# First modulation in blocks of 256 channels, part of its sums on VectorE, projection 0 started block by block, and the context's modulation vector made apart

## The chip, the cores and the metric

The kernel runs on one core of a Trainium2 chip. The metric is the device time of one execution in microseconds (us). Engines are named as in the profile: PE is TensorE (PEld its weight loads), DVE VectorE, ACT ScalarE, POOL GpSimd, SP SyncE, which here only issues DMAs.

## What is computed

One layer of a diffusion backbone in float32, for 1024 latent positions and 256 context positions of 1024 channels. The part in question:

```python
mod = silu(c) @ w_mod + b_mod                 # (1024) @ (1024 x 6144)
sh1, sc1, g1, sh2, sc2, g2 = split(mod, 6)
mod_ctx = silu(c_ctx) @ w_mod + b_mod         # same weights, another vector
sh1c, sc1c = mod_ctx[:d], mod_ctx[d:2*d]      # only its first two sixths are used
h  = rms_norm(x,   norm_mix_w) * (1 + sc1)  + sh1
hc = rms_norm(ctx, norm_mix_w) * (1 + sc1c) + sh1c
proj = h @ w_in                               # q, k, v and the two GLU halves
kv_ctx = hc @ w_in[:, k and v columns]        # the context gives keys and values only
```

The GLU half of proj goes through a 31-tap depthwise convolution over positions, q, k and v through windowed attention with the context's keys; then the output projection, a gated residual, a second modulation, and an up and down projection with a width-3 convolution between.

## The kernel before

Engines run their own instruction lists and meet only at semaphores; the order within each list is written out by hand. Operands of the large products are float32 values split in a high part (rounded by ACT to the faster float32r form) and a low part (the difference, by DVE), and each product is hi*hi + hi*lo + lo*hi. hx holds both parts of h^T: 8 channel tiles k, parts 0 and 1, 1024 positions.

**First modulation.** w_mod's first 2048 columns (sh1 and sc1) are loaded as eight row tiles k of 1 MB (L435), between the tiles of x (L432). mod_item(k) (L567) multiplies the 16 column blocks of tile k by natw, in which the vectors of latent and context alternate (L1036), so that one product gives both. The 128 products (fp32, two records each in the trace) accumulate in PSUM banks 0 to 3; tiles 0 to 2 stand ahead of the transposes of x, tile 3 between its two halves, 4 to 7 behind them. When all eight are done, DVE adds the bias and makes the factors A1 = (1 + sc1) * norm weight and modl = sh1, and Ac and modc for the context (L1056, L1059).

**h.** x is squared and summed by ACT (L813), scaled by the inverse root by DVE (L1025), both halves of four row tiles, turned by PE (L553), and copied out of PSUM by DVE (first half, L1041) and ACT (second, L818) to xnT. Then for each k ACT writes the high part (L846), DVE rewrites xnT with the modulated value (L1067) and subtracts (L1070): h_lo counts these.

**Projections 0 to 7** are the GLU columns in blocks of 128 (L601 to L605): 48 matmuls of 512 columns each, in PSUM banks 2 * (n % 4) and the next. Projection 0 follows h_lo step by step, the others wait for their split weights (gw_lo, made by DVE at L1029 from ACT's L831), and from the fifth on for banks that DVE has read (u_done). Every second projection DVE makes a gated product u (L1098) from PSUM and a sigmoid of ACT. Between, DVE works through the taps of the convolution (L234 to L260; TAP_GLU says how many after each projection: 11, 11, 13, 13, 13, 13, 6), one channel tile of four is done as products of ACT (L208) which POOL's DMAs add up (L216). DVE also splits the QKV weights, one k at a time (L1033). The context is turned inside projection 1 (L563), copied by ACT (L861), and modulated behind it by ACT (L866) and DVE (L1087, L1089).

**QKV projection** (L773, L774): ten position tiles, two of the context first; it starts when all eight QKV weight splits (qw_lo) and the context's low part (hc_lo) are there. Attention and the rest follow. Beside attention POOL makes the other four sixths of the modulation: it multiplies a row tile of w_mod by the vector (L519) and adds it to a sum by a DMA that accumulates (L527); PE sums over partitions at the end (L738).

## Time and profile before

| | before |
|---|---|
| median of 3 runs | 1194.03 us (1193.31 to 1195.86) |
| span of the profiled execution | 1198.3 us |
| PE busy | 1135.2 us, 95% |
| PEld busy | 964.9 us, 81% |
| DVE busy | 935.2 us, 78% |
| ACT busy | 575.3 us, 48% |
| POOL busy | 291.1 us, 24% |
| mean granted clock of PE | 0.979 |

The profile is of one execution, which spans 4.3 us more than the median of the runs. A slice of the page's picture is 30 us; the change lies in the first six. Rows of order of time give the start, the length from the first start to the last end, engine, line, operation, and in brackets how long the engine had been idle and what released it. Lengths of neighbouring instructions overlap a little, so spacing counts more than length.

### The profile page before, as it was taken

To read this page: it belongs to the slowest core of one execution; us is meant where nothing else is said; L and a number is where in the kernel's file an instruction comes from. 1 tells how busy PE (TensorE), PEld (TensorE's weight loads), DVE (VectorE), ACT (ScalarE), POOL (GpSimd) and SP (SyncE) were. 2 spreads that over 40 slices of the span, in tenths; PEclk is the share of its full clock that TensorE was granted. 3 is DMA by queue.
4 is the path that set the end of the run, shared out by engine and by line. 5 is a ranking of instruction groups with operands and counts; after the bars stand their busy time and mean duration, and the time that the engine had idled before them with its cause. 6 is when DMAs were issued, how large, how long until landed. Compare 5 with 4: busy or idle time off the path is not lost.

```text
span 1198.3 us, 17077 instructions
## 1 busy us (share of the span) xinstructions
PE 1135.2 (95%) x5953; PEld 964.9 (81%) x5953; DVE 935.2 (78%) x1426; ACT 575.3 (48%) x983; POOL 291.1 (24%) x331
## 2 busy tenths in 40 slices
PE   6899999989999999998799999999999999999996
PEld 6877788889898887786688878787878878888885
DVE  3269988769897664459999999999999875867763
ACT  4352346756565765555444434343434444444441
POOL 2100011115454100002545454455410020000111
PEclk9899999989998999999899999999999999999999
DMA  9321555619999414213445454545433284443474
GB/s 368 133 76 61 127 106 108 122 54 233 251 261 258 141 53 158 106 64 94 139 147 169 142 169 129 175 127 184 130 119 105 89 285 171 115 115 97 119 164 70
DMA packets 103090, 171.77 MB, mean 143 GB/s; under 512 B 9322, under 2 KB 62690, under 8 KB 102004
## 3 DMA queue, kind: packets, MB, share of 16 engines
q1 hardware_dynamic: 82388, 104.70, 26.5%
q0 software_dynamic: 20640, 66.27, 23.4%
q8 instruction: 37, 0.61, 0.2%
q14 instruction: 25, 0.20, 0.1%
HBM read 112.21 MB, written 31.46 MB: 120 GB/s over the span
## 4 chain that ended last, share of the span: by engine, by line
PE 39%; DVE 13%; issue 6%; ACT 5%; DVEq 0%; ACTq 0%; POOL 0%
PE ps L1610 16%; PE ps L1660 6%; PE ps L1661 6%; PE ps L1662 6%; PE ps L1575 5%; DVE y L2026 3%; DVE w_op L1927 3%; DVE w_raw L1945 2%; DVE y L2022 2%; ACT w_op L1731 1%; ACT y L1819 1%; DVE u L2015 1%; DVE s_sum L1945 1%; ACT h_second L1724 0%; PE ps L1586 0%
## 5 line engine op out<-in xcount | busy, mean ns | idle before, releaser
L1610 PE MATMUL ps<-t_op,w_op 128*128 128x512 f32 x1056 | 248.1, 390 | 3.8 <-DVE cv L2015 1.7
L1610 PEld LDWEIGHTS ps<-t_op,w_op 128*128 128x128 f32 x1056 | 197.2, 188 | 49.1 <-issue 6.3
L1610 PE MATMUL ps<-hx,w_op 128*128 128x512 f32 x792 | 191.5, 395 | 9.7 <-DVE u L2015 7.0
L1610 PEld LDWEIGHTS ps<-hx,w_op 128*128 128x128 f32 x792 | 150.5, 191 | 43.6 <-DVE u L2015 6.5
L1731 ACT ACTIVATE w_op<-w_raw 128x512 fp32r<-128x512 f32 x132 | 79.9, 622 | 197.3 <-DVE w_raw L1945 184.6
L1660 PE MATMUL ps<-dnh,ah 128*128 128x512 f32 x308 | 120.1, 390 | 1.6 <-DVE dnl L2033 1.6
L1661 PE MATMUL ps<-dnl,ah 128*128 128x512 f32 x308 | 119.9, 389 | 0.0
L1662 PE MATMUL ps<-dnh,al 128*128 128x512 f32 x308 | 119.8, 389 | 0.0
L1927 DVE TENSOR_TENSOR w_op<-w_raw,w_op 128x512 fp32r<-128x512 f32 x132 | 100.6, 777 | 9.9 <-ACT w_op L1731 8.0
L1839 ACT ACTIVATE ah<-hid 128x512 fp32r<-128x512 f32 x77 | 48.6, 632 | 116.6 <-PE ps L1662 112.5
L2033 DVE TENSOR_TENSOR al<-hid,ah 128x512 fp32r<-128x512 f32 x77 | 53.2, 691 | 48.6 <-ACT ah L1839 47.8
L690 PE MATMUL ps<-vraw,pt 128*128 128x64 f32 x608 | 81.5, 281 | 7.7 <-ACT pt L996 7.6
L2171 POOL DMA_DIRECT2D wd<-in_w_down x44 | 32.0, 729 | 227.9 <-DVE h_first L1916 159.7
L690 PEld LDWEIGHTS ps<-vraw,pt 128*128 128x128 f32 x608 | 77.5, 200 | 11.0 <-ACT pt L996 8.2
L1575 PE MATMUL ps<-wo_op,hx 128*128 128x512 f32 x336 | 79.4, 392 | 0.3 <-PEq L348 0.3
L1575 PEld LDWEIGHTS ps<-wo_op,hx 128*128 128x128 f32 x336 | 62.4, 188 | 14.1 <-issue 1.1
L1660 PEld LDWEIGHTS ps<-dnh,ah 128*128 128x128 f32 x308 | 57.8, 188 | 14.5 <-DVE dnl L2033 2.4
L2177 POOL TENSOR_TENSOR wd<-wd 128x256 f32<-128x256 f32 x44 | 48.9, 1112 | 77.4 <-DMA wd<-in_w_down 75.6
L1662 PEld LDWEIGHTS ps<-dnh,al 128*128 128x128 f32 x308 | 57.8, 188 | 12.0
L1661 PEld LDWEIGHTS ps<-dnl,ah 128*128 128x128 f32 x308 | 57.8, 188 | 11.9
L1189 DVE TENSOR_REDUCE scal<-ps 128x1 f32<-128x640 f32 (+1 forms) x64 | 50.2, 785 | 19.8 <-PE ps L661 10.7
L927 ACT ACTIVATE p<-ps,scal,msq 128x640 f32<-128x640 f32 (+1 forms) x60 | 51.8, 863 | 18.9 <-DVE scal L1192 16.7
(288 smaller groups left out, 2381.9 us busy)
## 6 DMA issues: line engine op xcount, KB each, us to landing
w_raw<-in_w_up SPq DMA_DIRECT2D x44, 512.0 KB, 5.1
wm<-in_w_mod SPq DMA_DIRECT2D x32, 512.0 KB, 6.3
sums<-wm POOLq DMA_DIRECT2D x32, 512.0 KB, 7.9
wd<-in_w_down POOLq DMA_DIRECT2D x44, 256.0 KB, 3.3
w_down_sums<-wd POOLq DMA_DIRECT2D x44, 256.0 KB, 2.8
dn_raw<-w_down_sums SPq DMA_DIRECT2D x44, 256.0 KB, 2.6
hid_scratch<-hid SPq DMA_DIRECT2D x20, 512.0 KB, 4.0
hid<-hid_scratch POOLq DMA_DIRECT2D x20, 512.0 KB, 5.8
```

The costliest lines, as they stand in the source:

```text
L690: last = pe.matmul(ps[:, 6, hl * HD:(hl + 1) * HD], pt[:, it % NPT, hl * P:(hl + 1) * P], vraw[:, kts[j], g, :], start=(j == 0 and hl == 0 ...
L927: act.activation(probs(n)[:, hl, 0:w], score_ap(hh, w), ACT.Exp, scale=msq[:, CT + n // NG, GQ * (n % NG) + hl:GQ * (n % NG) + hl + 1], bi ...
L1189: dve.reduce_max(s[:, 0, hl:hl + 1], score_ap(hh, w), axis=AX.X, negate=True).then_inc(max_done, 1)
L1575: last = pe.matmul(ps[:, b + hh, :], a, wo_half(k, lo, hh), start=(k == 0 and v == 0 and lo == 0), stop=(k == KT - 1 and v == 1))
L1610: last = pe.matmul(bank_of(p, s), w_op[p][w][:, k, :], rows_of(p, k, v), start=(start and k == 0 and w == 0 and v == 0), stop=(k == KH - 1 ...
L1660: pe.matmul(o, ah[b][:, c_], dnh[b][:], start=start, stop=False, skip_group_check=True)
L1661: pe.matmul(o, ah[b][:, c_], dnl[b][:], start=False, stop=False, skip_group_check=True)
L1662: return pe.matmul(o, al[b][:, c_], dnh[b][:], start=False, stop=(i == NK2 - 1), skip_group_check=True)
L1731: act.activation(w_op[p][0][:], w_part(s, p), ACT.Copy).then_inc(up_hi, 1)
L1927: dve.tensor_tensor(out=w_op[p][1][:], in0=w_part(s, p), in1=f(w_op[p][0][:]), op=ALU.subtract).then_inc(up_lo, 1)
L2033: dve.tensor_tensor(out=lo[n % 3][:], in0=src, in1=f(hi[n % 3][:]), op=ALU.subtract).then_inc(dn_split, 1)
L2177: pool.tensor_tensor(out=o, in0=a, in1=b, op=ALU.subtract).then_inc(wd_step, 1)
```

## The change

- Loads: all of x first; w_mod's first 2048 columns come as four blocks i of 256 channels (both the shift's and the scale's columns of them, all 1024 rows), each in four DMAs.
- For block i DVE multiplies row tiles 0 to 4 by the vector and sums them in macc (mod_part, five operations of 128 x 512); PE multiplies tiles 5 to 7 by natw as before (mod_direct, 12 matmuls) and adds the partition sum of macc (mod_rest, 4 matmuls). natw holds the latent's vector alone. mod_add makes the factors of the block's two channel tiles.
- As soon as a block's factors stand, h is made for its two k: ACT the high part, POOL the modulated value (into h32, the place of the low part), DVE the low part, and PE does these two steps of projection 0 ahead of the next block's mod_rest. ACT's split of the second weight block moves in between the h of k = 5 and of k = 6.
- The second half of x is scaled by POOL, not DVE.
- The context's vector is made apart: its 16 row products of 1024 by POOL (cwm), added up by 14 accumulating DMAs (csum), loaded by SP between the GLU weights; ctx_columns gives the partition sums on PE in projection 5, step 6; its factors and modulation are made by DVE and ACT behind that projection (n == 5 and 6), not at n == 2.
- ACT's tap product 1 waits for the accumulation and product 2 for ctx_columns, whose memory they use; PE banks and semaphores are renumbered; u's fourth tile is cleared later.

The diff, cut to its core:

```diff
+                wmk = w_mod[0].rearrange("(k p) n -> p k n", p=P)
+
+                def load_mod(i):
+                    for h in range(2):
+                        for s in range(2):
+                            c0 = s * D + i * 2 * P
+                            sp.dma_start(wm[:, i, h * KT // 2:(h + 1) * KT // 2, s, :],
+                                         wmk[:, h * KT // 2:(h + 1) * KT // 2, c0:c0 + 2 * P]).then_inc(wm_in[i][h], 16)
+
+                def load_cmod(k):
+                    for a in range(2):
+                        n = 2 * (k % 2) + a
+                        if k >= 2:
+                            sp.wait_ge(mod_acc[a], 16 * (k - 2)) if k > 2 else sp.wait_ge(mod_mul, a + 1)
+                        sp.dma_start(cwm[n][:], w_mod[0, k * P:(k + 1) * P, a * D:(a + 1) * D]).then_inc(wm2_in[n], 16)
...
+                    for k in ((1,), (2,), (3, 4), (5, 6), (7,), (), (), ())[n]:
+                        load_cmod(k)
...
+                pool.wait_ge(ms_rst, 4)
+                for t in range(*BATCHES[1]):
+                    pool.tensor_scalar(xs[:, t, :], xs[:, t, :], rst[:, t:t + 1], 1.0, ALU.mult, ALU.mult).then_inc(h_mod, 1)
                 pool.wait_ge(xT, 2 * KT)
-                pool.memset(u[:], 0.0).then_inc(const_done, 1)
+                pool.memset(u[:, 0:3, :], 0.0).then_inc(const_done, 1)
+                pool.wait_ge(xT_lo, KT)
+                pool.wait_ge(xT_out, KT)
+                for k in range(KT):
+                    pool.wait_ge(ab_done, 2 * (k // 2) + 2)
+                    pool.tensor_scalar(h32[:, k, 1, :], xnT[:, k, :], A1[:, k:k + 1], modl[:, k:k + 1], ALU.mult, ALU.add).then_inc(h_mod, 1)
+
+                pool.wait_ge(h_hi, KT)
+                for k in range(KT):
+                    for a in range(2):
+                        n = 2 * (k % 2) + a
+                        pool.wait_ge(wm2_in[n], 16 * (k // 2 + 1))
+                        pool.tensor_scalar((cwm[n] if k else csum[a])[:], cwm[n][:], nat[:, k, 1:2], 1.0, ALU.mult, ALU.mult).then_inc(mod_mul, 1)
+                        if k:
+                            pool.wait_ge(mod_mul, 2 * k + a + 1)
+                            pool.wait_ge(mod_mul, a + 1)
+                            if k > 1:
+                                pool.wait_ge(mod_acc[a], 16 * (k - 1))
+                            pool.dma_start(csum[a][:], cwm[n][:], accum_op=ALU.add).then_inc(mod_acc[a], 16)
+                pool.wait_ge(mod_acc[1], 16 * (KT - 1))
+                pool.memset(u[:, 3, :], 0.0).then_inc(const_done, 1)
...
+                def mod_direct(i):
+                    pe.wait_ge(wm_in[i][1], 32)
+                    if i == 0:
                         pe.wait_ge(silu_done, 3)
+                    for j in range(4):
+                        for k in range(DIRECT, KT):
+                            pe.matmul(ps[:, mod_bank(i), j * P:(j + 1) * P], wm[:, i, k, j // 2, j % 2 * P:(j % 2 + 1) * P], natw[:, k, :],
+                                      start=(j == 0 and k == DIRECT), stop=False, skip_group_check=True)
+
+                def mod_rest(i):
+                    pe.wait_ge(macc_done, DIRECT * (i + 1))
+                    for j in range(4):
+                        last = pe.matmul(ps[:, mod_bank(i), j * P:(j + 1) * P], macc[i % 2][:, j * P:(j + 1) * P], ones[:],
+                                         start=False, stop=True, skip_group_check=True)
+                    last.then_inc(mod_mm, 1)
...
+                def ctx_columns():
+                    for a in range(2):
+                        pe.wait_ge(mod_acc[a], 16 * (KT - 1))
+                    pe.wait_ge(u_done, 2)
                     for j in range(2 * KT):
-                        last = pe.matmul(ps[:, j // 4, j % 4 * P:(j % 4 + 1) * P], wm[:, k, j * P:(j + 1) * P], natw[:, k, :],
-                                         start=(k == 0 and j % 4 == 0), stop=(k == KT - 1), skip_group_check=True)
+                        last = pe.matmul(ps[:, CCOL_BANK, j * MOD_W:(j + 1) * MOD_W], csum[j // KT][:, j % KT * P:(j % KT + 1) * P], ones[:, 0:MOD_W],
...
+                mod_direct(0)
+                mod_rest(0)
+                mod_direct(1)
+                pe.wait_ge(gw_lo, 1)
+                for i in range(NPAIR):
+                    for k in range(2 * i, 2 * i + 2):
+                        glu_step(0, k)
+                    if i + 1 < NPAIR:
+                        mod_rest(i + 1)
+                    if i + 2 < NPAIR:
+                        mod_direct(i + 2)
...
+                    if k == KT - 2:
+                        split_glu(1)
...
+                def mod_part(i, k):
+                    src = wm[:, i, k].rearrange("p s n -> p (s n)")
+                    dst = macc[i % 2][:]
+                    dve.wait_ge(wm_in[i][2 * k // KT], 32)
+                    if k == 0:
+                        if i >= 2:
+                            dve.wait_ge(mod_mm, i - 1)
+                        dve.tensor_scalar(dst, src, nat[:, k, 0:1], None, ALU.mult).then_inc(macc_done, 1)
+                    else:
+                        dve.wait_ge(macc_done, DIRECT * i + k)
+                        dve.scalar_tensor_tensor(out=dst, in0=src, scalar=nat[:, k, 0:1], in1=dst, op0=ALU.mult, op1=ALU.add).then_inc(macc_done, 1)
+
+                def mod_add(i):
+                    by_pair = lambda ap: ap.rearrange("p (s k) -> p s k", s=2)[:, :, 2 * i:2 * i + 2]
+                    dve.wait_ge(mod_mm, i + 1)
+                    src = ps[:, mod_bank(i), :].rearrange("p (s k w) -> p s k w", s=2, w=P)[:, :, :, 0]
+                    dve.tensor_tensor(out=by_pair(modl), in0=src, in1=by_pair(cols[:, C_BMOD:C_BMOD + 16]), op=ALU.add).then_inc(ab_done, 1)
+                    dve.wait_ge(ab_done, 2 * i + 1)
+                    dve.scalar_tensor_tensor(out=A1[:, 2 * i:2 * i + 2], in0=modl[:, KT + 2 * i:KT + 2 * i + 2], scalar=1.0,
+                                             in1=cols[:, C_NMIX + 2 * i:C_NMIX + 2 * i + 2], op0=ALU.add, op1=ALU.mult).then_inc(ab_done, 1)
+
+                def h_low(k):
+                    dve.wait_ge(h_hi, k + 1)
+                    dve.wait_ge(h_mod, TT // 2 + k + 1)
+                    dve.tensor_tensor(out=hx[:, k, 1, :], in0=h32[:, k, 1, :], in1=f(hx[:, k, 0, :]), op=ALU.subtract).then_inc(h_lo, 1)
...
+                for i in range(NPAIR):
+                    for k in range(DIRECT):
+                        mod_part(i, k)
+                        if i and k in (1, 3):
+                            h_low(2 * i - 2 + k // 2)
+                    mod_add(i)
+                    if i == 0:
+                        split_glu(0)
...
+                    if n == 6:
+                        dve.wait_ge(ab_done, 2 * NPAIR + 2)
                         for k in range(KT):
                             dve.wait_ge(h_hi, KT + k + 1)
-                            dve.tensor_scalar(hc32[:, k, :], hc32[:, k, :], Ac[:, k:k + 1], modc[:, k:k + 1], ALU.mult, ALU.add).then_inc(h_mod, 1)
-                        dve.wait_ge(h_mod, 2 * KT)
-                        dve.tensor_tensor(out=hcx[:, :, 1, :], in0=hc32[:], in1=f(hcx[:, :, 0, :]), op=ALU.subtract).then_inc(hc_lo, 1)
+                            dve.tensor_scalar(hc32[:, k, 1, :], hc32[:, k, 1, :], Ac[:, k:k + 1], modc[:, k:k + 1], ALU.mult, ALU.add).then_inc(h_mod, 1)
```

## Rows read from the trace of the kernel before

**Rows 1.** Stretches: length, busy PE PEld DVE ACT POOL, clock, DMA; then PE's waits.
```profile
160.00:200.00 40.00, 40.00 (x249) 35.37 (x248) 34.45 (x90) 22.52 (x45) 6.78 (x8) 1.00 0.56 106
...
PE ps L601 <- DVE gwl L1029: 2.1, 2, 1.5
```

**Rows 2.** PE in order of time: start, length, line, count, idle time before.
```profile
6.38 9.75 PE L572 MATMUL ps<-natw,wm 128*128 128x128 f32 x64 [3.49 <-DMA wm<-in_w_mod]
...
21.92 4.49 PE L553 MATMUL ps<-ident,xs 128*128 128x128 f32 x32 [0.58 <-DVE xs L1025]
...
29.02 6.77 PE L572 MATMUL ps<-natw,wm 128*128 128x128 f32 x32 [2.28 <-DMA wm<-in_w_mod]
...
39.37 14.46 PE L572 MATMUL ps<-natw,wm 128*128 128x128 f32 x128
58.94 0.62 PE L601 MATMUL ps<-hx,gwh 128*128 128x512 f32 x1 [5.11 <-DVE hx L1070]
...
61.48 0.63 PE L601 MATMUL ps<-hx,gwh 128*128 128x512 f32 x1
...
120.81 0.50 PE L601 MATMUL ps<-hx,gwh 128*128 128x512 f32 x1 [0.57 <-DVE gwl L1029]
...
153.76 0.39 PE L774 MATMUL ps<-qwh,hcx 128*128 128x256 f32 x1
```

**Rows 3.** DVE in order of time, the last low half and second weight block.
```profile
69.86 1.22 DVE L1072 TENSOR_TENSOR hx<-xnT,hx 128x1024 fp32r<-128x1024 f32 x1
...
71.06 1.22 DVE L1029 TENSOR_TENSOR gwl<-gw_raw,gwh 128x1024 fp32r<-128x1024 f32 x1
```

**Rows 4.** DVE in order of time, from the first gated product on.
```profile
85.86 1.22 DVE L1098 TENSOR_TENSOR u<-ps,u 128x1024 f32<-128x1024 f32 x1 [5.55 <-PE ps L605]
...
90.26 0.74 DVE L249 SCALAR_TENSOR_TENSOR cacc<-conv_v,scal,cacc 128x512 f32<-128x512 f32 x1
...
95.58 2.67 DVE L1087 TENSOR_SCALAR hc<-hc,scal 128x256 f32<-128x256 f32 x8
98.28 2.29 DVE L1089 TENSOR_TENSOR hcx<-hc,hcx 128x2048 fp32r<-128x2048 f32 x1
...
109.79 1.22 DVE L1098 TENSOR_TENSOR u<-ps,u 128x1024 f32<-128x1024 f32 x1
...
151.88 1.82 DVE L1033 TENSOR_TENSOR qwl<-qw_raw,qwh 128x768 fp32r<-128x768 f32 x2
```

**Rows 5.** ACT in order of time, the start.
```profile
11.97 1.06 ACT L813 ACTIVATE junk<-xs 128x1024 f32<-128x1024 f32 x1 [8.80 <-DMA xs<-in_x]
...
17.38 1.28 ACT L825 ACT_TABLE_LOAD   x1
...
54.44 5.77 ACT L846 ACTIVATE hx<-xnT,scal 128x1024 fp32r<-128x1024 f32 x5 [13.20 <-DVE scal L1059]
```

**Rows 6.** Two stretches of 2 us, columns as in the first group.
```profile
30.00:32.00 2.00, 2.00 (x12) 2.00 (x11) 1.97 (x12) 0.00 (x0) 0.00 (x0) 0.50 1.02 422
60.00:62.00 2.00, 2.00 (x6) 1.52 (x6) 2.00 (x3) 2.00 (x3) 0.00 (x0) 0.50 0.02 4
```

**Rows 7.** POOL and DVE at 316 us in order of time; L519 and L249 min/median/max ns.
```profile
316.76 1.42 POOL L519 TENSOR_SCALAR wm<-wm,scal 128x1024 f32<-128x1024 f32 x1
...
316.82 1.91 DVE L249 SCALAR_TENSOR_TENSOR conv_a<-u,cols,conv_a 128x513 f32<-128x513 f32 x1
...
L519 POOL TENSOR_SCALAR wm<-wm,scal x32: 1108/1117/2299, 267.1 to 392.6; 128x1024 f32<-128x1024 f32 x32
...
L249 DVE SCALAR_TENSOR_TENSOR conv_a<-u,cols,conv_a x45: 741/746/1908, 88.9 to 350.7; 128x513 f32<-128x513 f32 x45
```

**Rows 8.** PE's weight loads in order of time, the column sums of L738.
```profile
424.93 1.86 PEld L738 LDWEIGHTS ps<-ones,sums 128*128 128x128 f32 x16
```

**Rows 9.** DMA issues: count, KB each, us from issue to landing.
```profile
sums<-wm POOLq DMA_DIRECT2D x32, 512.0 KB, 7.9
...
conv_y<-u POOLq DMA_DIRECT2D x10, 512.0 KB, 4.5
```

More of the change, by code:

```diff
@@ L453, in _ @@
+                sp.dma_start(qkw[:, 0, :], q_norm_w[0].partition_broadcast(P)).then_inc(small_in, 16)
+                sp.dma_start(qkw[:, 1, :], k_norm_w[0].partition_broadcast(P)).then_inc(small_in, 16)
+                sp.wait_ge(xT, 2 * KT)
+                load_cmod(0)
                 for n in range(NGL):
-                    if n + 1 < NGL:
+                    if n and n + 1 < NGL:
                         sp.wait_ge(gw_lo, n + 1)
@@ L539, in vectors @@
                     for v, n in enumerate((N_A - 2 * KT, 4 * FT, 4 * FT, TAPS * CTL)):
-                        last = pe.transpose(ps[:, 7, off:off + n], vecs[0:n, v, :], ident[0:n, 0:n])
+                        last = pe.transpose(ps[:, VEC_BANK, off:off + n], vecs[0:n, v, :], ident[0:n, 0:n])
                         off += n
@@ L574, in mod_item, with glu_step @@
                     last.then_inc(mod_mm, 1)
-                for k in range(3):
-                    mod_item(k)
+                def glu_step(n, k):
+                    b = 2 * (n % 4)
+                    if n == 0:
+                        pe.wait_ge(h_lo, k + 1)
+                    for hh in range(2):
+                        o, s = ps[:, b + hh, :], slice(hh * HALF, (hh + 1) * HALF)
+                        pe.matmul(o, gwh[:, n % 2, k, :], hx[:, k, 0, s], start=(k == 0), stop=False)
+                        pe.matmul(o, gwh[:, n % 2, k, :], hx[:, k, 1, s], start=False, stop=False)
+                    for hh in range(2):
+                        o, s = ps[:, b + hh, :], slice(hh * HALF, (hh + 1) * HALF)
+                        last = pe.matmul(o, gwl[:, n % 2, k, :], hx[:, k, 0, s], start=False, stop=(k == KT - 1))
+                    if k == KT - 1:
+                        last.then_inc(gl_mm, 1)
@@ L834, in split_qkv @@
                     act.wait_ge(qw_in[k % 2], 16 * (k // 2 + 1))
+                    if k == 5:
+                        for a in range(2):
+                            act.wait_ge(mod_acc[a], 16 * (KT - 1))
                     act.activation(qwh[:, k, :], qw_raw[:, k % 2, :], ACT.Copy).then_inc(qw_hi, 1)
@@ L848, in _ @@
                     square(t)
-                split_glu(1)
-                act.wait_ge(ms_done, 3)
+                act.wait_ge(ms_rst, 5)
                 act.activation(rst[:, TT:TT + CT], ss[:, TT:TT + CT], ACT.Sqrt).then_inc(sqrt_done, 1)
@@ new lines, in h_low, with mean_squares @@
+                def h_low(k):
+                    dve.wait_ge(h_hi, k + 1)
+                    dve.wait_ge(h_mod, TT // 2 + k + 1)
+                    dve.tensor_tensor(out=hx[:, k, 1, :], in0=h32[:, k, 1, :], in1=f(hx[:, k, 0, :]), op=ALU.subtract).then_inc(h_lo, 1)
+                def mean_squares(r):
+                    t0, t1 = BATCHES[r]
+                    dve.wait_ge(sq_done, t1)
+                    dve.tensor_scalar(ss[:, t0:t1], ss[:, t0:t1], 1.0 / D, EPS, ALU.mult, ALU.add).then_inc(ms_rst, 1)
```

206 lines of the change are left out of this document (103 added, 103 removed).

## The prediction, made before the change was built

> **What bounds the kernel now.** I read the page first: PE is busy for most of the span, but the first slices are thin, and what the diff touches lies ahead of 160 us. So I read stretches and waits [rows 1], then PE, DVE and ACT in order of time. All this is one profiled execution of 1198.3 us span; the median of the runs is 1194.03. Each step below shifts a moment against the same moment of that execution, and the sum is added to the median.
>
> Three parts matter. *Start:* PE modulates as data lands; its last 128 records begin at 39.37 and take 14.46 us; the first projection step starts at 58.94 [rows 2], paced by DVE, whose last low half (1.22 us) begins at 69.86. The second weight block's split begins at 71.06 and takes 1.22 [rows 3], so projection 1 begins at about 72.85 (end of that and of projection 0). *Strip:* from 85.86, the first gated product, DVE works without a gap until the last projection weights are split, 151.88 + 1.82 = 153.70 [rows 4]; PE waits twice for it in there, 2.1 us together [rows 1]. The QKV projection starts at 153.76 [rows 2], released by that split. *After it* PE is full, 40.00 us of 40 from 160 to 200 [rows 1]. So the end moves with the QKV projection's start, and DVE's strip sets this, not PE's eight projections alone.
>
> **Part 1, the order of loads.** The first megabyte lands by 6.38 [rows 2]; now it is x. From ACT's first square to the end of the fourth is 17.38 - 11.97 = 5.4 us with a short wait for data, so 5.0; from there to the first transpose 21.92 - 17.38 = 4.5 [rows 2, 5]. Transposes begin at 6.4 + 5.0 + 4.5 = 15.9, 6.0 earlier than at 21.92. Then the gain is spent. PE has idled before them, and rows show what that does: after 2.28 us idle it is at 0.50 of its clock (1.2 of 2.4 GHz) at 30 to 32, after 5.11 us idle again at 60 to 62 [rows 2, 6]. Half clock lasts 3.4 us (matmuls stay 0.43 apart from 58.94 to 62.3) to some 6.2 (nearly the whole row of 6.77 at 29.02) [rows 2]. Eight transposes take 4.49 us at full clock; bounds 4.49 and 9; I take 6.2, to 22.1. The second half of the rows is now scaled by POOL behind DVE's sixth copy (about 21.5): four operations of the form whose median is 1.12 us [rows 7], 4.5, and 1.4 for two that meet part 2's sums: 27.4. Eight more transposes behind an idle PE, same bounds, I take 5.6: 33.0. Then mod_direct(0) and mod_rest(0), 16 matmuls or 32 records: 14.46 / 4 = 3.6 at full clock, 6.77 at half [rows 2]; I take 3.8, and 0.6 for the small DVE steps (53.83, where PE ended, to ACT's first high half at 54.44) [rows 5]. The first factors stand at 37.4 instead of 54.4. Bounds: 33.6 (full clock throughout) and 43.
>
> **Part 2, the blocks.** PE's 29 us of modulation become 4 x 3.8, but each block is now a chain over four engines. DVE: five sums over 512 columns, at 0.74 us for the tap form of that size [rows 4] and less for the first, a plain product: 3.4, of which the last lies beside PE. Two low halves, 1.16 apart: 2.3. Then, since mod_rest stands behind two projection steps, 6 matmuls at full clock (an eighth of a projection; three took 153.76 - 120.81 = 32.95 [rows 2], so 1.37), 8 records (0.9), 0.5 on DVE. 7.8 us a block.
>
> Unknown is POOL's share. It makes eight scaled copies while DVE makes sums with two SBUF inputs. [rows 7] show such a pair: the sum of 513 columns, median 0.746 us, took 1.91 when it began beside POOL's tensor_scalar. It lost 1.16, the whole of such a POOL operation: the two took turns. In a gapless stream I price each POOL operation at 1.05 us; bounds 0 (it hides in DVE's waits) and 1.16. That is 2.1 more a block, 9.9. Three blocks and split_glu(0) (1.14): 37.4 + 1.1 + 29.7 = 68.2 for the fourth factors. The Trainium skill ("SBUF — State Buffer", section "SBUF: two separate sides") says that VectorE and GpSimd share one port pair as an exclusive lock, held for the whole instruction, also between a VectorE operation with two SBUF inputs and a GpSimd one that reads SBUF. By that rule each would cost its full 1.1; [rows 7] agree.
>
> Then ACT splits the second weight block ahead of the last pair's high halves: with a low half 1.06 + 1.15 + 1.16 = 3.5 us in which PE has nothing, 4 with the step before. So the last two projection steps start at half clock: 61.48 - 58.94 = 2.54 us for six matmuls [rows 2]. With part of the second step at full clock, projection 1 begins 8.3 after the factors, at 76.5: 3.7 us *later* than at 72.85. Bounds 64.4 and 82.
>
> **Part 3, the context's vector.** Its modulation, 2.67 + 2.29 or 4.9 us of DVE, moves from behind projection 1 to behind the fifth [rows 4]. The strip holds it either way. But where it stood it filled a hole: without it DVE stands at the second gated product (before at 109.79) at 104.9, and PE delivers that block only at 107.5; 2.8 us idle. The context columns are 32 records; [rows 8] give 1.86 for 16, so 3.6 us inside projection 5, just ahead of the third gated product, which DVE awaits: 2.9 idle. With 0.5 of small steps the strip grows by 6.2 even if POOL costs nothing; the two PE waits of 2.1 vanish in it.
>
> POOL's 16 products of context rows: two fall in the last low halves, four while DVE waits for projection 1, ten in the strip ahead of the third gated product, 10.5 us. That leaves of the idle times none and 2.4. Strip: 10.5 + 0.5 + 2.4, I take 13.5 longer. Queued behind POOL's waits for the accumulations are only its own next products and a memset; SP's next context rows wait for them too, and ACT's second tap product. At the 4.5 us of the product ring the chain ends near 130, and PE asks at 138; at 7.9 it ends near that [rows 9].
>
> **PE's clock at the QKV projection.** PE ends projection 7 two projections (21.9) behind the third gated product's start, DVE its last split 21.5 + 4.9 behind it: PE idles 4.7 us, then runs at half clock for 3.4 to 6.2: 1.7 to 3.1 lost, I take 2.4. Nothing gives it back while PE is full.
>
> **Sum.** +3.7 (start) + 13.5 (strip) + 2.4 (clock) = +19.6; 1194.0 + 19.6 = 1213.6, I say 1213.
>
> **Rivals.** (a) POOL beside DVE costs nothing. For it: I saw few meetings. Against: the 1.91. The start comes 6.3 earlier and the strip grows by 6.2, not 13.5: 1200. (b) Faster: PE, not DVE's strip, sets the QKV start, so the start's gain is kept. With full clock and no port cost projection 1 begins at 64.4 (-8.4), the columns add 3.6, the two waits save 2.1: -6.9, 1187. It decides where DVE reaches the third gated product more than 4.9 us ahead of PE. Against it: the gapless strip. (c) The early start of (b) with the strip of (a): -8.4 + 6.2 and up to 2.4 for the clock: 1191.8 to 1194.2, the same; this is the change not doing what it is for. (d) Slower still: accumulations at 7.9 us, so PE and ACT wait for the context's sums, or all transposes at half clock: 1222 to 1235.
>
> **How the numbers follow.** Forecast 0.57 (1204 to 1222), (a) 0.15 (1197 to 1204), (b) 0.08, (c) 0.08, (d) 0.12. A measurement of this kernel can tell about 0.2%, 2.4 us. Leaving out (b), (c) and the far third of (d) gives 1198 to 1226. Faster 0.08, same 0.08, slower 0.84.
>
> **What would show it.** Transposes from about 16; block 0's factors at 37 and the others 10 us apart (8 in rival (a)); DVE's sums stretched to 1.4 to 1.9 beside each POOL tensor_scalar; clock 0.50 around the last two steps of projection 0 and at the QKV start; the last split at about 171. It is wrong if projection 1 begins before 67, or if the strip from the first gated product to the last split is under 75 us (67.8 before).

## The result: 37 us slower, and where they are

| | before | after |
|---|---|---|
| median | 1193.67 us (4 runs, 1192.09 to 1195.86) | 1231.07 us (4 runs, 1225.45 to 1237.27) |
| ratio, 95% interval | | 1.0319 [1.0286, 1.0351] |
| profiled execution | 1198.3 us span, clock 0.979 | 1235.5 us span, clock 0.965 |
| first gated product (DVE) | 85.86 | 91.02 |
| last QKV weight split ends, QKV projection starts | 153.7 | 188.4 |
| strip between these two | 67.8 | 97.4 |
| from there to the end | 1044.6 | 1047.1 |

The forecast was 1213 with a range to 1226. It was right in sign and missed the range: 5.2 us were lost up to the first gated product (forecast 3.7), 29.6 in DVE's strip (forecast 13.5), 2.5 behind it (forecast 2.4). So nearly all that was missed lies in the strip. The agreement behind it counts for little: the part from the QKV start to the end differs by 10 us between executions of one kernel (shown below), and the kernel before was profiled in a long execution. Times run 1.8 us above spans; by the median of its runs its remainder would be about 1038, not 1044.6, and that of the changed kernel 1041.

DVE of the changed kernel in order of time (start, length, line, count, idle time before and its releaser), from the first gated product to the last QKV split; it answers to [rows 4]:

```profile
91.02 1.23 DVE L1229 TENSOR_TENSOR u<-ps,u 128x1024 f32<-128x1024 f32 x1 [5.53 <-PE ps L662]
...
101.40 1.54 DVE L259 SCALAR_TENSOR_TENSOR cacc<-conv_v,scal,cacc 128x512 f32<-128x512 f32 x1
102.86 2.43 DVE L259 SCALAR_TENSOR_TENSOR conv_a<-u,cols,conv_a 128x513 f32<-128x513 f32 x1
105.21 2.43 DVE L259 SCALAR_TENSOR_TENSOR conv_b__88<-u,cols,conv_b__88 128x512 f32<-128x512 f32 x1
107.57 0.74 DVE L259 SCALAR_TENSOR_TENSOR cacc<-conv_v,scal,cacc 128x512 f32<-128x512 f32 x1
...
115.84 1.23 DVE L1126 TENSOR_TENSOR gwl<-gw_raw,gwh 128x1024 fp32r<-128x1024 f32 x1 [3.55 <-ACT gwh L921]
...
136.84 1.23 DVE L1126 TENSOR_TENSOR gwl<-gw_raw,gwh 128x1024 fp32r<-128x1024 f32 x1 [5.04 <-ACT gwh L921]
...
156.63 0.17 DVE L1209 TENSOR_TENSOR scal<-ps,cols 128x16 f32<-128x16 f32 x1 [4.53 <-PE ps L648]
...
161.98 1.23 DVE L1229 TENSOR_TENSOR u<-ps,u 128x1024 f32<-128x1024 f32 x1 [4.97 <-PE ps L662]
...
186.61 1.82 DVE L1130 TENSOR_TENSOR qwl<-qw_raw,qwh 128x768 fp32r<-128x768 f32 x2
```

Two kinds of loss are to be seen. Idle time: 3.55 + 5.04 for GLU weights that come late (L1126), 4.53 for the context's columns (L1209) and 4.97 for the gated product behind them, 18.1 in all; before there was none. And longer sums. The groups by line in the same stretch (busy us, mean ns; the 62 tap sums of L259):

```profile
L259 DVE SCALAR_TENSOR_TENSOR conv_a<-u,cols,conv_a 128x513 f32<-128x513 f32 x22 | 21.5, 975 | 0.0
L259 DVE SCALAR_TENSOR_TENSOR cacc<-conv_v,scal,cacc 128x512 f32<-128x512 f32 x20 | 18.1, 907 | 0.0
L259 DVE SCALAR_TENSOR_TENSOR conv_b__88<-u,cols,conv_b__88 128x512 f32<-128x512 f32 x20 | 17.4, 872 | 0.0
```

57.0 us; 62 sums at the 0.742 of the kernel before are 46.0, so 11.0 went to turns with POOL, against 10.5 in the forecast (how they came about is taken up behind the experiments). 18.1 + 11.0 leave 0.5 for the small steps.

POOL in the same stretch (its tensor_scalar are the row products, DMA_DIRECT2D its issue of an accumulating DMA), some of the list and its end:

```profile
80.81 0.95 POOL L564 DMA_DIRECT2D csum<-cwm  x1 [0.31 <-POOL cwm L558]
...
97.19 5.21 POOL L558 TENSOR_SCALAR cwm<-cwm,scal 128x1024 f32<-128x1024 f32 x1 [3.72 <-DMA cwm<-in_w_mod]
102.70 0.87 POOL L564 DMA_DIRECT2D csum<-cwm  x1 [0.30 <-POOL cwm L558]
103.32 1.43 POOL L558 TENSOR_SCALAR cwm<-cwm,scal 128x1024 f32<-128x1024 f32 x1
...
129.21 2.05 POOL L558 TENSOR_SCALAR cwm<-cwm,scal 128x1024 f32<-128x1024 f32 x1 [0.86 <-DMA cwm<-in_w_mod]
135.01 0.88 POOL L564 DMA_DIRECT2D csum<-cwm  x1 [3.76 <-DMA csum<-cwm]
...
142.65 0.88 POOL L564 DMA_DIRECT2D csum<-cwm  x1 [0.39 <-POOL cwm L558]
150.74 0.98 POOL L566 MEMSET u<- 128x1066 f32 x1 [7.21 <-DMA csum<-cwm]
```

The first accumulation is issued at 80.81, the last has landed just ahead of 150.74: seven rounds in 69.9 us, 10.0 each. PE's columns start when it has, in the middle of projection 5, after 2.45 us of waiting, and most of them run at half clock (5.81 instead of the 3.6 of the forecast). The granted clock stays at 0.50 until 162, which is why DVE waits 4.97 us for the gated product behind them, and 2.54 in a kernel without the accumulations, whose clock is full there. PE in order of time:

```profile
117.12 0.50 PE L658 MATMUL ps<-hx,gwh 128*128 128x512 f32 x1 [4.44 <-DVE gwl L1126]
...
138.12 0.80 PE L658 MATMUL ps<-hx,gwh 128*128 128x512 f32 x1 [8.21 <-DVE gwl L1126]
...
150.78 5.81 PE L648 MATMUL ps<-ones,csum 128*128 128x32 f32 x32 [2.45 <-issue]
...
188.49 0.58 PE L864 MATMUL ps<-qwh,hcx 128*128 128x256 f32 x1 [4.55 <-DVE qwl L1130]
```

What a round of 10 us is made of stands in the DMA issues from 86 to 160 us (count, KB each, median us from issue to landing):

```profile
csum<-cwm POOLq DMA_DIRECT2D x12, 512.0 KB, 8.3
cwm<-in_w_mod SPq DMA_DIRECT2D x10, 512.0 KB, 6.7
gw_raw<-in_w_in SPq DMA_DIRECT2D x4, 512.0 KB, 9.2
```

and in SP's waits from 80 to 160 us (sum, times, longest):

```profile
SPq L468 <- DMA csum<-cwm: 42.6, 10, 7.7
```

The accumulations take 8.3 us, a GLU weight block 9.2, and SP stands 42.6 us at L468, where a row's load waits for the accumulation that frees its buffer; the next GLU weights are queued behind it. The stretches of 20 us from 90 to 150 (columns as in [rows 1]) show DMA share at 0.97 to 1.00 and PE's clock falling with its waits:

```profile
90.00:110.00 20.00, 20.00 (x89) 16.53 (x89) 18.94 (x22) 2.99 (x4) 11.99 (x8) 1.00 0.97 252
110.00:130.00 20.00, 15.47 (x60) 11.98 (x58) 16.45 (x19) 1.79 (x2) 10.37 (x10) 0.91 1.00 264
130.00:150.00 20.00, 10.21 (x36) 7.96 (x36) 14.96 (x17) 6.98 (x7) 6.39 (x6) 0.83 0.99 251
```

The profile alone doesn't say which of the three holds the strip: late weights, turns, or the chain of accumulations (each adds to the sum that the one before it left). Each hides the others. The experiments take them away one at a time.

### The profile page after: what moved, and what is told of

It is laid out like the page before. It is cut to its first block, busy times and chain, and to the rows that moved or that the text cites. A ratio compares the mean times of both kernels' runs of the same rounds, so it can differ in the third digit from the quotient of the medians.

```text
span 1235.5 us, 17013 instructions
## 1 busy us (share of the span) xinstructions
PE 1134.8 (92%) x5857; PEld 964.8 (78%) x5857; DVE 962.5 (78%) x1440; ACT 576.0 (47%) x983; POOL 350.6 (28%) x374
## 4 chain that ended last, share of the span: by engine, by line
PE 31%; DVE 16%; issue 8%; ACT 6%; DVEq 1%; ACTq 0%; POOL 0%
PE ps L1741 9%; PE ps L1791 5%; PE ps L1793 5%; PE ps L1792 5%; PE ps L1706 5%; DVE y L2157 4%; DVE w_op L2058 3%; DVE w_raw L2076 2%; DVE y L2153 2%; ACT w_op L1862 2%; ACT y L1950 2%; DVE u L2146 1%; DVE s_sum L2076 1%; DVE scal L2188 0%; ACT h_second L1855 0%
## 5 line engine op out<-in xcount | busy, mean ns | idle before, releaser
L658 PE MATMUL ps<-hx,gwh 128*128 128x512 f32 x128 | 55.4, 433 | 25.3 <-DVE hx L1156 12.7
L1706 PEld LDWEIGHTS ps<-wo_op,hx 128*128 128x128 f32 x336 | 62.4, 188 | 14.1 <-issue 1.1
L2308 POOL TENSOR_TENSOR wd<-wd 128x256 f32<-128x256 f32 x44 | 46.3, 1052 | 72.1 <-DMA wd<-in_w_down 70.3
L1320 DVE TENSOR_REDUCE scal<-ps 128x1 f32<-128x640 f32 (+1 forms) x64 | 50.3, 786 | 19.0 <-PE ps L751 10.4
```

The source lines that it names most:

```text
L658: pe.matmul(o, gwh[:, n % 2, k, :], hx[:, k, 0, s], start=(k == 0), stop=False)
L1320: dve.reduce_max(s[:, 0, hl:hl + 1], score_ap(hh, w), axis=AX.X, negate=True).then_inc(max_done, 1)
L1706: last = pe.matmul(ps[:, b + hh, :], a, wo_half(k, lo, hh), start=(k == 0 and v == 0 and lo == 0), stop=(k == KT - 1 and v == 1))
```

## The experiments

Each ratio is against runs of the kernel before on the same chip at the same time; the landmarks are those of one profiled execution. "Rest" is from the end of the strip to the end. The changed kernel and the one with PE busy at the QKV door are the same code up to that door, and their strips are 97.4 and 95.5: steps of 2 us between strips mean nothing, those of 6 and more do.

| kernel | median us | ratio, 95% | first gated | strip | QKV starts | rest |
|---|---|---|---|---|---|---|
| before | 1190.99 to 1193.67 | | 85.86 | 67.8 | 153.7 | 1044.6 |
| start alone | 1202.37 | 1.0089 [1.0060, 1.0117] | 88.25 | 67.8 | 156.1 | 1039.0 |
| start alone, ACT for POOL | 1199.49 | 1.0077 [1.0046, 1.0108] | 88.00 | 67.8 | 155.9 | 1041.7 |
| start alone, PE kept busy | 1195.22 | 1.0033 [1.0013, 1.0053] | 88.16 | 67.9 | 156.0 | 1035.5 |
| one context row | 1208.59 | 1.0156 [1.0101, 1.0210] | 90.90 | 74.2 | 165.1 | 1043.0 |
| products, no accumulations | 1217.72 | 1.0235 [1.0191, 1.0279] | 88.99 | 81.9 | 170.9 | 1042.5 |
| short accumulations | 1220.80 | 1.0260 [1.0216, 1.0303] | 89.55 | 86.0 | 175.6 | 1038.9 |
| accumulations, no products | 1228.72 | 1.0320 [1.0280, 1.0360] | 88.57 | 95.2 | 183.8 | 1042.7 |
| after | 1231.07 | 1.0319 [1.0286, 1.0351] | 91.02 | 97.4 | 188.4 | 1047.1 |
| rows loaded from POOL's queue | 1232.63 | 1.0351 [1.0321, 1.0382] | 89.54 | 99.3 | 188.8 | 1042.4 |
| after, PE busy at the QKV door | 1226.74 | 1.0306 [1.0260, 1.0352] | 89.64 | 95.5 | 185.1 | 1040.0 |
| POOL adds, no DMA | 1243.66 | 1.0418 [1.0380, 1.0455] | 93.43 | 106.3 | 199.8 | 1042.6 |
| POOL adds, PE kept busy | 1237.12 | 1.0381 [1.0353, 1.0409] | 91.37 | 103.9 | 195.2 | 1037.5 |

**The start alone.** Context rows, products, accumulations and ctx_columns go out; the context is modulated at n == 2 again, with the latent's vector.

```diff
-                    if n == 5:
-                        dve.wait_ge(mod_mm, NPAIR + 1)
-                        dve.tensor_tensor(out=modc, in0=ps[:, CCOL_BANK, :]...
+                    if n == 1:
+                        dve.tensor_copy(modc, modl).then_inc(ab_done, 1)
```

> The new start alone: the context uses the latent's vector (so the context's own vector is left out: no rows loaded for it, no POOL products, no accumulations, no column sums) and is modulated behind projection 1 as in the kernel before. Theory 'strip' (most of the 37 us comes from what the context's vector does behind projection 1): projection 1 begins at 77 to 78 as in the changed kernel, 5 us later than before, DVE's strip is 67.8 us again with PE never idle at the QKV projection's door: 1198 to 1200. Rival 'start' (the new start disturbs more than the moment at which projection 1 begins): 1205 or more.

The first gated product came 2.4 us late, and the strip was 67.8 us, that of the kernel before to a tenth: what the start costs in front of the strip is passed on whole, and nothing of the strip's growth is the start's. The median, however, was 9.9 us above, between the 1198 to 1200 of 'strip' and the 1205 of 'start'. Where the rest of it lies is taken up at the end of this section.

**Late weights taken away.** POOL loads rows 2 to 7 itself, each right behind the wait that frees its buffer, so SP never waits for an accumulation.

```diff
-                    for k in ((1,), (2,), (3, 4), (5, 6), (7,), (), (), ())[n]:
-                        load_cmod(k)
+                    if n == 0:
+                        load_cmod(1)
```

> The changed kernel whole, but the context's rows k = 2 to 7 are loaded from POOL's queue, so that SP's queue never waits for an accumulation ahead of a GLU weight load. Theory 'queue' (SP's waits make the weights of projections 4 and 5 late; DVE idles 3.6 and 5.0 us for them, PE 4.4 and 8.2, and PE falls to half clock before the column sums): the two idle times go, column sums take 3.6 instead of 5.8 us, the strip falls from 97 to about 82 us, 1214 to 1219. Rival 'turns' (DVE and POOL taking turns is the whole cause, the late weights are only a symptom of POOL's slowness): within 3 us of the changed kernel, 1228 or more.

The late weights went, as both ideas wanted: PE's waits for a split fell from 4.44 + 8.21 to 0.56 + 1.44. The time did not. What came in their place, among PE's and DVE's waits of this run (sum, times, longest):

```profile
PE ps L651 <- issue: 18.4, 1, 18.4
DVE scal L1212 <- PE ps L651: 18.3, 1, 18.3
```

PE reached ctx_columns 18.4 us ahead of the context's sums, and stood. The sums were ready at the same moment as in the changed kernel (the memset behind them began at 151.16; 150.74 in the changed kernel). So the 'queue' theory falls: SP's blocked queue had only hidden the chain. The rival, 'turns', had its number (at or over 1228), but not for its reason, as the next run shows.

**Turns taken away.** POOL multiplies one column of 1024 for rows 1 to 7 (the rest of the product is left out); the loads and all accumulations stand.

```diff
+                        w = 1 if k else D
-                        pool.tensor_scalar((cwm[n] if k else csum[a])[:], cwm[n][:], ...
+                        pool.tensor_scalar((cwm[n] if k else csum[a])[:, 0:w], cwm[n][:, 0:w], ...
```

> The changed kernel, but for k from 1 to 7 POOL multiplies one column of 1024 instead of all (the context's vector is therefore not the reference's); loads, accumulations and all waits stay. Theory 'turns': the 10.9 us by which DVE's sums are stretched in the strip go, and with POOL's products the chain of accumulations is shorter, so SP's waits shrink too: 10.9 plus 5 to 9, so 1211 to 1215. Theory 'queue' alone (turns hide in idle time): only the chain's shortening counts, 1220 to 1226.

The tap sums were short again (16.4, 14.9 and 14.9 us for the 62), so 11 us of DVE's work had gone, and the median was 1228.7, above both numbers on record: nearly nothing came back. The 16.0 us that DVE now stood for GLU weights took its place:

```profile
L259 DVE SCALAR_TENSOR_TENSOR conv_a<-u,cols,conv_a 128x513 f32<-128x513 f32 x22 | 16.4, 748 | 0.0
...
L1127 DVE TENSOR_TENSOR gwl<-gw_raw,gwh 128x1024 fp32r<-128x1024 f32 x5 | 6.1, 1219 | 16.0 <-ACT gwh L922 16.0
```

Both of these theories had been mine, and both fell. What the three runs share is the end of the accumulations, 147.4 to 151.2. The theory from here on: the chain of seven accumulations per half holds the strip, and late weights and turns only fill the time in front of it.

**One context row.** No chain, no turns, but the late place and the columns as in the change. Rows 1 to 7 are left out.

```diff
-                for k in range(KT):
+                for k in range(1):
```

> The changed kernel, but the context's sums are left at their first row: GpSimd loads and multiplies row 0 alone, rows 1 to 7 are neither loaded, multiplied nor accumulated (that part of the context's vector is left out). The start, the 16 column matmuls inside projection 5 and the late modulation of the context stand. Theory 'chain' (the seven accumulations per half, one behind the other, end at 150.7 us and hold the columns, everything else only hides in front of them): the strip from the first gated product to the last QKV split falls from 97.3 to 75-79 us (67.8 before, plus 2.8 at the second gated product, 3.6 to 5.8 of columns on TensorE and up to 2.4 behind them), the QKV stage starts near 167, the time is 1207-1213. Rival 'order' (the late place of the context's vector, its modulation and the start cost it, whoever adds the rows): strip 85 or more, time 1218 or more.

**All products, no accumulations.** Loads and products stand, only row 0 reaches the sums. What waited for an accumulation (SP's next rows, PE's columns, ACT) now waits for products.

```diff
-                            pool.dma_start(csum[a][:], cwm[n][:], accum_op=ALU.add).then_inc(mod_acc[a], 16)
-                pool.wait_ge(mod_acc[1], 16 * (KT - 1))
+                pool.wait_ge(mod_mul, 2 * KT)
```

> The changed kernel with all its 16 row loads and all 16 GpSimd products, but no accumulation: each product overwrites its row and only row 0 reaches the columns (the sum over the rows is left out). The turns between GpSimd and VectorE stand, the chain of accumulating DMAs is gone. Theory 'chain': strip 84-90 us (the one-row kernel plus the 10 or so us of turns that the forecast priced), time 1214-1220, so 11-17 under the changed kernel. Rival 'turns' (the products hold VectorE and SyncE's loads as much without the accumulations): strip 93 or more, time 1225 or more.

Both came as 'chain' said: 1208.6 with a strip of 74.2 (a little below the 75 to 79 expected) and 1217.7 with 81.9 (84 to 90 expected). The steps add up: the late place costs 6.4 us of strip (2.67 idle at the second gated product, 0.56 and 2.54 around the columns, and small steps), the products 7.7, the accumulations 15.5. The last are 4.3 us by which DVE is busy for longer (79.1 instead of 74.8) and 11.1 by which it idles for longer (18.1 instead of 7.0): 8.6 for late GLU weights, 1.3 at the columns and 2.4 at the gated product behind them, less 1.2 at the second gated product. DVE's idle rows with one context row:

```profile
112.67 1.23 DVE L1219 TENSOR_TENSOR u<-ps,u 128x1024 f32<-128x1024 f32 x1 [2.67 <-PE ps L653]
135.70 0.17 DVE L1199 TENSOR_TENSOR scal<-ps,cols 128x16 f32<-128x16 f32 x1 [0.56 <-PE ps L639]
138.62 1.23 DVE L1219 TENSOR_TENSOR u<-ps,u 128x1024 f32<-128x1024 f32 x1 [2.54 <-PE ps L653]
```

**Short accumulations.** Every wait, load, product and DMA is there, but a DMA adds 64 of 1024 columns (the rest of the sum is left out).

```diff
-                            pool.dma_start(csum[a][:], cwm[n][:], accum_op=ALU.add)
+                            pool.dma_start(csum[a][:, 0:64], cwm[n][:, 0:64], accum_op=ALU.add)
```

> The changed kernel, but each accumulating DMA adds 64 of 1024 columns (1/16 of the bytes; the rest of the sum is left out); loads, products and waits are all as they were. Theory 'latency' (what an accumulation takes is fixed and the product in front of it is waited for): accumulations still end at 145 us or later and the time stays at 1226-1233. Rival 'bytes' (7 to 8 us is what 512 KB take to be read, added and written): the chain ends before 128 us, no wait for the columns, and the time is near the kernel with products and no accumulations, 1214-1220.

'Bytes' was right in the main, 'latency' wrong: the chain ended at 129.36 and the median was 1220.8, each just outside what 'bytes' gave (128, and 1214 to 1220) and far from 'latency' (145 or later, 1226 to 1233). DMA issues of this run, 86 to 160 us:

```profile
cwm<-in_w_mod SPq DMA_DIRECT2D x8, 512.0 KB, 5.6
gw_raw<-in_w_in SPq DMA_DIRECT2D x4, 512.0 KB, 3.9
...
csum<-cwm POOLq DMA_DIRECT2D x12, 32.0 KB, 2.9
```

32 KB were added in 2.9 us, 512 KB in 8.3, and with the bytes gone the GLU weights landed in 3.9 again instead of 9.2. The last sum was there ahead of 129.36, 21 us earlier, and PE didn't wait for it. So it is the traffic of the accumulations, seven rounds of it in sequence, not a fixed delay of each. The short DMAs leave 4.1 us of strip above the kernel without any: there the SP queue still stood 14.0 us for an accumulation.

**POOL adds.** If the DMA's bytes are the cost, POOL can add each product itself (nothing is left out).

```diff
-                            pool.dma_start(csum[a][:], cwm[n][:], accum_op=ALU.add).then_inc(mod_acc[a], 16)
+                            pool.tensor_tensor(out=csum[a][:], in0=cwm[n][:], in1=csum[a][:], op=ALU.add).then_inc(mod_mul, 1)
```

> The changed kernel, nothing left out, but GpSimd adds each product to the context's sum itself (14 additions of 1024 columns) instead of handing it to an accumulating DMA. Theory 'chain of DMAs': the loads land in 5 us again, the sums end before 140 us and the time is 1216-1224, the 1217.7 of products without accumulations plus a few us for 14 more turns with VectorE. Rival (a GpSimd addition of two SBUF operands beside VectorE's stream takes as long as the DMA it replaces, or holds VectorE more): sums end after 145 us, 1227 or more.

The rival had its number, and the time was even 13 us above the changed kernel's. POOL's groups by line in this run, 78 to 200 us, one of its rows in order of time, and DVE's first group, 85 to 200 us:

```profile
L561 POOL TENSOR_TENSOR csum<-cwm,csum 128x1024 f32<-128x1024 f32 x14 | 36.1, 2581 | 1.2
L558 POOL TENSOR_SCALAR cwm<-cwm,scal 128x1024 f32<-128x1024 f32 x14 | 22.3, 1591 | 12.2 <-DMA cwm<-in_w_mod 12.2
...
123.54 3.60 POOL L558 TENSOR_SCALAR cwm<-cwm,scal 128x1024 f32<-128x1024 f32 x1 [10.57 <-DMA cwm<-in_w_mod]
```
```profile
L259 DVE SCALAR_TENSOR_TENSOR conv_a<-u,cols,conv_a 128x513 f32<-128x513 f32 x22 | 24.3, 1102 | 0.0
```

An addition takes POOL 2.58 us, and DVE's sums rise to 1.10 us on the mean. The loads landed in 4.9 and the GLU weights in 4.0, so the traffic was gone, but the sums ended at 150.4 all the same, and the strip was 8.9 us longer than with the accumulating DMAs. Not all of that end is POOL's pace: ahead of 123.54 it stood 10.57 us for a row that SP issued only at 117.25, behind a GLU weight load that waited for DVE's split of 114.77. With its rows in time the sums would have been ready up to 10 us sooner (an estimate from that wait); this wasn't tried.

**PE's clock.** Three runs put matmuls that compute nothing in use where PE idles: 20 at the QKV door of the changed kernel, 4 ahead of each step of projection 0 in the start alone, and both in the kernel with POOL's additions.

```diff
+                for _ in range(20):
+                    pe.matmul(ps[:, 0, :], gwh[:, 1, 0, :], hx[:, 0, 0, 0:HALF], start=True, stop=True)
                 pe.wait_ge(qw_lo, KT)
```

> The changed kernel with 20 added matmuls of 512 columns into a free bank in front of TensorE's wait for the last QKV weight split (they compute nothing that is used). In the changed kernel TensorE idles 4.55 us there and the first 5.5 us of the QKV stage run at half clock, priced 2.4 us in the forecast. Theory: the stage starts at full clock and the time falls by 2 to 3 us, to 1228-1229. Rival: the clock falls elsewhere in its place or the queue of added matmuls delays the first real one, 1231 or more.

The changed kernel and this one at the door, stretches with PE busy, granted clock, DMA share, GB/s:

```profile
188.00:190.00 2.00, 1.51 (x7) 0.50 0.73 135
190.00:192.00 2.00, 2.00 (x11) 0.50 0.00 0
192.00:194.00 2.00, 2.00 (x15) 0.74 0.00 0
```
```profile
184.00:188.00 4.00, 3.70 (x27) 1.00 0.52 98
188.00:190.00 2.00, 2.00 (x19) 1.00 0.00 0
```

Half clock for 3.5 us of PE's work (1.2 of 2.4 GHz), and 0.74 for 2 more, was there, and is gone. The medians differ by 4.3 us, but the ratios, 1.0306 and 1.0319, overlap, and this execution reached the door 3.3 us sooner, which matmuls added at the door can't have brought. What it is worth in time isn't settled; from the rows it is 1.8 + 0.5, near the 2.4 of the forecast.

> The kernel with GpSimd's additions, with TensorE kept busy by added matmuls both in front of the steps of projection 0 (4 each) and at the door of the QKV stage (20): everything that the runs so far say can be had back of the change at once, with the right result. Theory: 4-8 us under the kernel with GpSimd's additions alone, 1210-1217, and still slower than the kernel before, since 14 us of the strip and the start's own chain stay. Rival: the two covers hide each other and it equals the kernel with the additions within 2 us.

The median fell by 6.5 us, as expected of the difference, but the intervals of the two ratios overlap; the 1210 to 1217 on record fell with the theory of the run before it, and 1237 stays 44 above the kernel before. I have no version that beats it. Taking the columns one projection later wasn't tried: csum lies in memory that a tap sum uses from then on.

**What of the start's 10 us is clock.**

Four matmuls stand ahead of each step's wait; ahead of the first, PE also waits for the copies of x^T out of PSUM.

```diff
+                        for _ in range(4):
+                            pe.matmul(ps[:, 2, :], gwh[:, 0, 0, :], gwh[:, 0, 0:4, :], start=True, stop=True)
                         pe.wait_ge(h_lo, k + 1)
```

> The start alone (the new start, but the context modulated early and with the latent's vector as in the first experiment, so that the context's own vector is left out), with 4 added matmuls of 512 columns in front of TensorE's wait for each of the eight steps of projection 0; they compute nothing that is used. The start alone took 1202.4 us against 1192.4, its runs between 1196 and 1206, the longer ones at a lower mean clock (0.974 against 0.983). Theory 'clock' (the new start leaves TensorE idle between blocks, which costs clock there, and this is what is left of its 9 us): 1193-1199. Rival 'order' (the start's cost is its chain of VectorE sums, factors and modulations, and the clock is only a trace of it): 1200-1205.

The 'clock' theory had its number: 1195.2, +3.3 parts in 1000 instead of +8.9, and the intervals are apart. But the first gated product came at 88.16, as without the added matmuls, so the gain isn't where I had put it. The start alone was therefore profiled three times more, to see one of its longer executions.

> The start alone once more, for a profile of one of its longer executions: its runs lay between 1196 and 1206 us at clocks of 0.985 to 0.974, and the one that was profiled was the second shortest. If the profiled execution takes over 1201 us, theory 'lost at the start' puts its first gated product at 91 us or later (88.25 in the short one) and the remainder behind the QKV stage's start at 1039-1041; rival 'lost later' leaves the first gated product at 88-89 and makes the remainder 1045 or more.

> The same kernel and the same question as the run before it: in an execution over 1201 us, the first gated product at 91 or later (lost at the start), or at 88-89 with a remainder of 1045 or more behind the QKV stage's start (lost later).

> The same kernel and the same question as the two runs before it: in an execution over 1201 us, the first gated product at 91 or later (lost at the start), or at 88-89 with a remainder of 1045 or more behind the QKV stage's start (lost later).

They took 1203.4, 1196.5 and 1206.8 us (the kernel before, once beside them, 1197.0). First gated products 89.84, 89.35, 89.51; strips 67.8 in all three; rest 1043.9, 1037.4 and 1047.7. 'Lost later' for 1206.8; 1203.4 stays just short of the 1045 that was asked for. The longest one and the shorter one (3) in the attention stage:

```profile
300.00:350.00 50.00, 47.78 (x352) 47.16 (x351) 40.48 (x68) 24.36 (x53) 27.61 (x26) 0.82 1.04 263
```
```profile
300.00:350.00 50.00, 47.14 (x416) 46.45 (x416) 45.63 (x86) 31.16 (x69) 23.09 (x23) 1.00 1.02 255
```

Clock 0.82 against 1.00 over 50 us, and 352 matmuls against 416. The part of the clock not granted, times PE's busy time, comes to 8.6 us in this stretch, against a difference of 10.4 between the two executions (an estimate). So at the start itself 2.4 to 4.0 us are lost, and the remainder of the 10 looks to be clock that executions lose more or less of in the attention stage, 200 us later. The rest from the QKV start on ran from 1035.5 to 1047.7 over all profiled executions, that of the kernel before (1044.6) among the long ones. Why the start makes the long ones more frequent, and added matmuls in projection 0 less so, is open.

> The changed kernel, but ACT instead of POOL makes the eight modulated copies at the start (part of the start only, the rest is as changed). If turns with POOL cost 1.5 to 2 us per block, as the stretched sums (1.3 to 1.5 and 1.7 instead of 0.74) suggest, blocks come 8.3 to 8.7 us apart instead of 9.7 and projection 1 begins about 74.5 instead of 78; ACT's two more operations of 1.15 us per block take part of it back. 3 us less: 1227 to 1229. If the turns hide in waits, 78 stays or grows to 80: 1231 to 1234.

By mistake this kernel was built on the start alone, not on the changed kernel as its expectation says: ACT instead of POOL makes the eight modulated copies, and the context's own vector is left out. So it is to be compared with the start alone: 1.0077 against 1.0089, intervals overlapping, first gated product 88.00 against 88.25. Moving the copies to ACT shifts work, and wins nothing that can be measured; its expectation of the whole change wasn't tested. Its part on the blocks was: no sum of the start was stretched (0.75 each), and yet blocks came 9.4 us apart (factors at 36.27, 45.74, 55.13 and 64.52), not the 8.3 to 8.7 expected.

## Why the prediction missed, step by step

- **Transposes from 15.9, factors at 37.4:** 16.84 and 37.69 in the changed kernel. Right.
- **Blocks 9.9 apart:** 12.5 for the first, then 9.7 and 9.7 (factors at 37.69, 50.15, 59.84, 69.52). The number is right but for the first block, in which PE ran at half clock from 43 to 49; its make-up isn't. The forecast was 7.8 without POOL's turns and 2.1 for them. With POOL's copies moved to ACT the turns were gone, and blocks were still 9.4 apart. How much of that is ACT's two added operations wasn't separated, but as far as the run tells, the 7.8 was too low, the 2.1 too high, and the sum lucky.
- **Projection 1 at 76.5 (+3.7):** near 78; the first gated product was 5.2 late in the changed kernel, 2.4 to 4.0 with the start alone. Within its bounds.
- **Turns, 1.05 us for each POOL operation, 10.5:** 11.0 in the changed kernel, but made up otherwise. Of the ten products one (111.93) fell where DVE idled. Each of the other nine stretched one sum: five sums by 0.8 us, and four by 1.7, those that began while POOL was issuing an accumulating DMA just ahead of its product, as at 102.86 (POOL's rows 102.70 and 103.32). In the kernel with products and no accumulations DVE's sums lost 5.8 and another tap 0.8, so 0.7 for each of ten. The price lies between two sizes, and that 10.5 met 11.0 is in part luck; the rival at no cost falls. All nine sums ended 0.53 to 0.55 us behind the product's end. The Trainium skill ("SBUF — State Buffer", section "SBUF: two separate sides") has the two engines exclude each other for a whole instruction; these ends agree with it. The same section of the Trainium skill gives the ports to whichever instruction starts first, and there the four long sums differ: each is recorded 0.45 us ahead of its product and still ended behind it. The issue alone doesn't stretch a sum (none is, with one-column products); why the two together do is open.
- **The late place, +6.2 of strip:** +6.4 with one context row. Right.
- **The strip without the chain, +13.5:** +14.1 in the kernel with products and no accumulations, whose QKV projection starts 17.2 us late, the 3.7 + 13.5 of the forecast. Luck again: the products cost DVE 6.6 instead of 10.5, and its idle times were 7.0 (1.21, 3.21 and 2.54) instead of 2.4. Its median is 27 above all the same; what is more than 17 lies behind the QKV start, where executions differ by 12 us.
- **The chain, priced at nothing.** Here the forecast failed: "At the 4.5 us of the product ring the chain ends near 130, and PE asks at 138; at 7.9 it ends near that". It ended at 150. Three things were wrong in that sentence. The duration was 8.3, not 4.5: the row at hand for accumulations that run beside loads, 7.9 [rows 9], had been kept as the bound. A round is more than its accumulation: of the twelve issues from 89.56 on, six waited for the accumulation ahead of them and six for their own product, four of these for a row that came late, as a load waits for its buffer and for SP's queue; 10.0 us a round, where even 7.9 would have had the chain done near 136. And the sentence compared the chain's end with a request of PE at 138, though the accumulations' own traffic made GLU weights late (9.2 instead of 4.0 us) on the way: PE asked at 148.3, so the waits for weights hid most of the wait for the chain. It is rival (d), to which I gave 0.12, and past its upper end of 1235 in one run. The cost is 15.5 us of strip.
- **The waits behind it.** I had named SP's next rows and ACT's product as queued behind the accumulations and left them at nothing. SP stood 42.6 us with GLU weights behind it, for which DVE idled 8.6.
- **Half clock at the QKV door, 2.4:** there, 2.3 by the rows, behind 4.55 us of idle time (the forecast's 21.5 + 4.9 - 21.9 is 4.5, not 4.7). Its time isn't settled. The half clock of the columns, 152 to 162, wasn't in the forecast.

By medians, 9.9 of the 37 us came with the start, 8 with the late place, 9 with the products and 11 with the accumulations. Each median is known to 3 to 7 us, and how much of the start's is clock is open; the strips, 6.4, 7.7 and 15.5, tell the last three apart better.

## What to carry to other kernels

A chain of DMAs that add into one buffer is priced by its round: load, product, accumulation and the wait that frees the buffer, with the durations of a stretch in which loads run beside it. Its end is then held against the moment at which its reader asks.

Where three waits lie one in front of the other, taking away one that ends earlier shows nothing; take away the one that ends last, and look at what its reader waits for.

Work given to POOL beside a gapless DVE isn't free even where POOL has nothing else to do: here a product of 1.1 us cost DVE 0.7 to 1.2 us on the mean.

## What the runs showed of the hardware

- An accumulating DMA of 512 KB took 8.3 us beside other loads, one of 32 KB 2.9. While the large ones ran, GLU weight loads of 512 KB took 9.2 (7.4 to 8.7 in three other kernels with them) instead of 3.9 to 4.1. The row loads' 6.7 isn't their mark: without accumulations, four issued one behind the other, they took 7.7.
- POOL's product of 128 x 1024, 1.1 to 1.4 us by itself, took 5.21 (at 97.19) beside a gapless row of DVE sums, of which only the last was stretched; its addition of two SBUF operands 2.58, and DVE's sums then 1.10 on the mean instead of 0.75.
- From the QKV start on the same kernel took 1037.4 to 1047.7 us in four executions, with PE's clock in a 50 us stretch of attention between 0.82 and 1.00.
